# mLSTM values and output gates as one level of Strassen's product, with the 404-column group first

## What is computed

```python
hin = _rms_norm(x, norm_g[0])
z = hin @ w_in
(mq, mk, mv, lq, lk, lv, lo, li, lf,
 nq, kc, vc, ksl, vsl, kwn, vwn, ng) = jnp.split(z, split_points, axis=-1)
...
qk = jax.nn.silu(_causal_conv(jnp.concatenate([lq, lk], axis=-1), conv_w, conv_b))
```

## Time and profile before

| what | value |
|---|---|
| median of 3 runs | 603.32 us (603.21 to 603.87) |
| the profiled execution, whole | 603.88 us |
| its span, first to last instruction | 602.1 us |
| PE busy | 590.5 us (98%), 3095 matmuls |
| DVE, ACT, POOL busy | 390.1, 300.0, 257.0 us |
| mean granted TensorE clock | 0.997 of full speed |

### The profile page before, as it was taken

The page is one execution under the profiler, slowest core; times in us unless marked ns, Lnnn a source line. Parts: engine busy times, 40 slices in busy tenths (PEclk is TensorE's granted clock), DMA queues, the critical chain, the costliest instruction groups (busy, mean ns, idle before and its releaser), DMA issues.

```text
span 602.1 us, 8286 instructions
## 1 busy us (share of the span) xinstructions
PE 590.5 (98%) x3095; PEld 484.5 (80%) x3095; DVE 390.1 (65%) x666; ACT 300.0 (50%) x529; POOL 257.0 (43%) x138
## 2 busy tenths in 40 slices
PE   8999999999999999999999999999999999999995
PEld 5898888877866678899878888888888888888884
DVE  6414605266978774983999777585595685771656
ACT  6713414654589934555645545444355265354322
POOL 7763323573094610043357443631723626611611
PEclk9999999999999999999999999999999999999998
DMA  8743282466023710028034340621603404104002
GB/s 326 288 144 137 72 208 71 87 161 208 1 45 104 264 63 0 1 72 280 1 143 137 136 144 1 209 71 67 202 12 139 141 0 153 57 1 175 1 35 106
DMA packets 36580, 67.18 MB, mean 112 GB/s; under 512 B 2876, under 2 KB 23612, under 8 KB 35516
## 3 DMA queue, kind: packets, MB, share of 16 engines
q1 hardware_dynamic: 36236, 66.25, 34.0%
q10 hardware_dynamic: 304, 0.39, 0.3%
HBM read 62.18 MB, written 2.10 MB: 107 GB/s over the span
## 4 chain that ended last, share of the span: by engine, by line
PE 89%; ACT 4%; DVE 3%; issue 2%; DMA 1%; SPq 0%; POOLq 0%; POOL 0%; ACTq 0%; DVEq 0%
PE ps L1814 19%; PE ps L1816 19%; PE ps L1815 19%; PE ps L2288 7%; PE ps L2290 7%; PE ps L2289 7%; PE ps L2140 2%; PE ps L2155 2%; PE ps L2051 1%; PE ps L2052 1%; ACT probs L949 1%; DMA x_land<-in_x_turned 1%; ACT W L890 1%; PE ps L1979 1%; PE ps L2216 1%
## 5 line engine op out<-in xcount | busy, mean ns | idle before, releaser
L1814 PE MATMUL ps<-xT_h,ring_h 128*128 128x512 f32 (+1 forms) x384 | 144.3, 376 | 0.3 <-DVE q_far L1361 0.3
L1816 PE MATMUL ps<-xT_h,ring_l 128*128 128x512 f32 (+1 forms) x384 | 143.2, 373 | 0.0
L1815 PE MATMUL ps<-xT_l,ring_h 128*128 128x512 f32 (+1 forms) x384 | 143.1, 373 | 0.0
L773 POOL TENSOR_TENSOR ring_l<-raw_d,ring_h 128x1024 fp32r<-128x1024 f32 x25 | 67.3, 2699 | 129.8 <-ACT ring_h L1044 129.8
L773 POOL TENSOR_TENSOR ring_l<-raw,ring_h 128x1024 fp32r<-128x1024 f32 x31 | 76.7, 2499 | 77.5 <-DVE xres L1630 38.1
L692 POOL TENSOR_TENSOR ring_l<-raw,ring_h 128x512 fp32r<-128x512 f32 (+2 forms) x26 | 64.2, 2489 | 74.1 <-ACT ring_h L796 74.1
L1724 DVE TENSOR_TENSOR y<-ps,y 128x512 f32<-128x512 f32 x90 | 61.2, 689 | 50.9 <-PE ps L2290 50.6
L1814 PEld LDWEIGHTS ps<-xT_h,ring_h 128*128 128x128 f32 x384 | 72.4, 188 | 14.0 <-issue 1.3
L1816 PEld LDWEIGHTS ps<-xT_h,ring_l 128*128 128x128 f32 x384 | 72.3, 188 | 12.9
L1815 PEld LDWEIGHTS ps<-xT_l,ring_h 128*128 128x128 f32 x384 | 72.4, 189 | 12.5
L2288 PE MATMUL ps<-ring_h,a_h 128*128 128x512 f32 x196 | 76.7, 391 | 0.1
(11 more groups left out here) (276 smaller groups left out, 994.7 us busy)
## 6 DMA issues: line engine op xcount, KB each, us to landing
raw<-in_w_mlp SPq DMA_DIRECT2D x16, 1024.0 KB, 5.6
raw_d<-in_w_mlp SPq DMA_DIRECT2D x16, 1024.0 KB, 6.1
raw<-in_w_groups SPq DMA_DIRECT2D x8, 1024.0 KB, 4.8
xres<-in_x SPq DMA_DIRECT2D x8, 512.0 KB, 6.3
raw<-in_nsa_cmp_w SPq DMA_DIRECT2D x8, 512.0 KB, 6.6
raw<-in_w_groups SPq DMA_DIRECT2D x8, 256.0 KB, 5.5
raw<-in_w_out SPq DMA_DIRECT2D x2, 1024.0 KB, 6.2
raw<-in_w_out SPq DMA_DIRECT2D x4, 512.0 KB, 4.8
```

What stands on the lines that cost most here:

```text
L773: nc.gpsimd.tensor_tensor(slot(ring_l, n), slot_source(n), slot(ring_h, n).bitcast(F32), ALU.subtract).then_inc(lo_done, 1)
L1814: nc.tensor.matmul(o, sh, mh, start=start, stop=False)
L1815: nc.tensor.matmul(o, sh, ml, start=False, stop=False)
L1816: return nc.tensor.matmul(o, sl, mh, start=False, stop=stop)
```

## The change

`lv` and `lo` are now one product of x (1024 features by 512 tokens) with 1024 columns, done by one level of Strassen's scheme in Winograd's form. x is cut in two halves of features and two halves of tokens (`x_part`), the weights in two halves of features and two of columns: `C_11` and `C_21` are `lv`, the raw halves of `lo` land in the chunks `C_T3` and `C_22`. Eight block products become seven (`C_11`, `C_T2`, `C_21`, `C_T3`, `C_T4`, `C_T1`, `C_22`), each of 2 token tiles by 4 slabs by 3 matmuls of 512 columns. That makes 168 matmuls in place of 192.

For that VectorE makes four sums of x blocks (`s_raw`, 128x1024) and ScalarE and VectorE their halves (`s_h`, `s_l`); VectorE makes four sums of weight blocks (128x2048, `weight_sum`), and it adds the products' banks (`first_p`, `two_p`, `three_p`) before the values are scaled and the gates are formed. Three of the seven chunks are not loaded but summed. Two further raw buffers are used, `raw2` and `raw3`, and two for sums, `t_sum`.

The first group, slab by slab, is now group B with 404 columns. `x_gain` writes x back where it lies in SBUF (`x_all`), so that ScalarE's rounding and `x_low` read SBUF too; `xf` is gone. The row of scales moves on TensorE from behind group B to behind the first convolution tile, and its bank from 3 to 7. POOL makes the low halves of `LQ` and `LK` before its small constants `sel`.

```diff
-SHARED = ()
-CHUNK_ORDER = [*range(C_MQ), C_CMP + 2, C_CMP + 3, *range(C_MQ, C_CMP + 2), *range(C_WO, C_MLP)]
+C_11, C_T2, C_21, C_T3, C_T4, C_T1, C_22 = range(C_S, C_S + 7)
+SUMMED = (C_T2, C_T4, C_T1)
+CHUNK_ORDER = [C_LK, C_11, C_T3, C_22, C_21, C_KVS, C_NQ, C_CMP + 2, C_CMP + 3, C_MQ, C_MK, C_CMP, C_CMP + 1, *range(C_WO, C_MLP)]
...
+    return {C_T2: 4, C_T1: 4, C_21: 2, C_22: 3, C_CMP: 1, C_CMP + 1: 0, C_CMP + 2: 2, C_CMP + 3: 3}.get(c, c % RAW)
...
+    if C_S <= c < C_KVS:
+        return (4 if c in (C_21, C_22) else 0), 4, [(LO if c in (C_T3, C_22) else LV, 512)]
...
+                if c in (C_21, C_22):
+                    sp.wait_ge(xl_ready, NC + 3)
...
+            low_half(C_LQ)
+            low_half(C_LK)
...
+                if c in (C_T1, C_T2, C_T3, C_T4):
+                    act.wait_ge(t_ready, (C_T1, C_T2, C_T3, C_T4).index(c) + 1)
+                else:
+                    act.wait_ge(raw_in[raw_slot(c)], raw_full(c))
...
-            high_half(2)
-            for t in range(NT):
-                x_root(t)
-            for c in (3, 4, 5, 6):
-                high_half(c)
+            high_half(C_LQ)
+            x_root(0)
+            x_root(1)
+            act.wait_ge(x_scaled, NC + 4)
+            for n in (1, 2, 0):
+                sum_high(n)
+            high_half(C_LK)
+            x_root(2)
+            x_root(3)
+            high_half(C_11)
...
-                    high_half(7)
+                    high_half(C_T2)
+            high_half(C_21)
             conv_sigmoid(3)
             act.wait_ge(*reads(J_B + NT - 1))
             nc.scalar.activation(gt[:], zB[:, :, BG:BG + 12], ACT.Sigmoid).then_inc(gates_ready, 1)
-            high_half(8)
-            for t in range(NT):
-                act.wait_ge(job_done, J_LO + t + 1)
-                act.wait_ge(x_rstd, t + 1)
-                nc.scalar.activation(y[:, t, 256:768], ps[:, (J_LO + t) % 8, :], ACT.Sigmoid,
-                                     scale=stat[:, R_X + t:R_X + t + 1]).then_inc(read_a, 1)
-            high_half(9)
+            high_half(C_T3)
+            high_half(C_T4)
+            high_half(C_T1)
+            act.wait_ge(job_done, J_S + 4)
+            sum_high(3)
+            high_half(C_22)
+            high_half(C_KVS)
+            high_half(C_NQ)
+            def gate_of(t, held):
+                nc.scalar.activation(y[:, t, 256:768], held, ACT.Sigmoid, scale=stat[:, R_X + t:R_X + t + 1])
+            act.wait_ge(x_rstd, NT)
+            for t in range(2):
+                act.wait_ge(part_read, 5 + t)
+                gate_of(2 + t, three_p[:, t, :])
+            for t in range(2):
+                act.wait_ge(*reads(J_S + 6 + t))
+                gate_of(t, two_p[:, t, :])
...
             def x_gain(k):
                 dve.wait_ge(x_land_in[k], 16)
-                if k == 0:
-                    dve.wait_ge(xf_ready, 1)
-                nc.vector.tensor_scalar(ps[:, 4 + k % 4, :], x_slab(k), gain_cols[:, k:k + 1], None, ALU.mult).then_inc(x_scaled, 1)
+                nc.vector.tensor_scalar(x_all[:, k, :], x_all[:, k, :], gain_cols[:, k:k + 1], None, ALU.mult).then_inc(x_scaled, 1)
             def x_low(k):
                 dve.wait_ge(xh_ready, k + 1)
-                nc.vector.tensor_tensor(xT_l[:, k, :], ps[:, 4 + k % 4, :], xT_h[:, k, :].bitcast(F32), ALU.subtract
+                nc.vector.tensor_tensor(xT_l[:, k, :], x_all[:, k, :], xT_h[:, k, :].bitcast(F32), ALU.subtract
                                         ).then_inc(xl_ready, 1)
+            def sum_low(n, order):
+                dve.wait_ge(xh_ready, NC + order)
+                nc.vector.tensor_tensor(s_l[n][:], s_raw[n][:], s_h[n][:].bitcast(F32), ALU.subtract).then_inc(xl_ready, 1)
             x_gain(0)
             for k in range(NC):
                 if k + 1 < NC:
                     x_gain(k + 1)
                 x_low(k)
+            nc.vector.tensor_tensor(s_raw[0][:], x_part(0, 1), x_part(1, 1), ALU.add).then_inc(x_scaled, 1)
+            nc.vector.tensor_tensor(s_raw[2][:], x_part(0, 0), x_part(0, 1), ALU.subtract).then_inc(x_scaled, 1)
+            dve.wait_ge(x_scaled, NC + 1)
+            nc.vector.tensor_tensor(s_raw[1][:], s_raw[0][:], x_part(0, 0), ALU.subtract).then_inc(x_scaled, 1)
+            dve.wait_ge(x_scaled, NC + 3)
+            nc.vector.tensor_tensor(s_raw[3][:], x_part(1, 0), s_raw[1][:], ALU.subtract).then_inc(x_scaled, 1)
+            for order, n in enumerate((1, 2, 0)):
+                sum_low(n, order + 1)
             for t in range(NT):
                 normalise(t)
+            link(nc.vector.memset(lv1[:, :, :, DV:DV + 1], 1.0))
...
+            def weight_sum(c):
+                if c == C_T1:
+                    dve.wait_ge(raw_in[raw_slot(C_11)], raw_full(C_11))
+                    dve.wait_ge(raw_in[raw_slot(C_T3)], raw_full(C_T3))
+                    dve.wait_ge(x_sq, NT)
+                    made = nc.vector.tensor_tensor(t_sum[0][:], raw[1][:], raw[0][:], ALU.subtract)
+                elif c == C_T2:
+                    dve.wait_ge(raw_in[raw_slot(C_22)], raw_full(C_22))
+                    dve.wait_ge(t_ready, 1)
+                    made = nc.vector.tensor_tensor(t_sum[1][:], raw[3][:, 0:CHUNK], t_sum[0][:], ALU.subtract)
+                elif c == C_T3:
+                    made = nc.vector.tensor_tensor(raw[1][:], raw[3][:], raw[1][:], ALU.subtract)
+                else:
+                    dve.wait_ge(raw_in[raw_slot(C_21)], raw_full(C_21))
+                    dve.wait_ge(t_ready, 2)
+                    dve.wait_ge(lo_done, split_no(C_11) + 1)
+                    made = nc.vector.tensor_tensor(raw[0][:], raw[2][:], t_sum[1][:], ALU.subtract)
+                made.then_inc(t_ready, 1)
...
+                if n == 0:
+                    weight_sum(C_T1)
+                if n == 1:
+                    weight_sum(C_T2)
+                if n == 2:
+                    weight_sum(C_T3)
             silu(3)
+            weight_sum(C_T4)
+            for t in range(2):
+                dve.wait_ge(part_used, 2)
+                nc.vector.tensor_copy(first_p[t][:], ps[:, t, :]).then_inc(part_read, 1)
+            for t in range(2):
+                dve.wait_ge(part_used, 3)
+                dve.wait_ge(part_read, 1 + t)
+                nc.vector.tensor_tensor(two_p[:, t, :], ps[:, 2 + t, :], first_p[t][:], ALU.add).then_inc(part_read, 1)
+            def values_of(t, bank):
+                return nc.vector.tensor_scalar(lv1[:, t, :, 0:DV], ps[:, bank, :].rearrange("p (h d) -> p h d", h=HEADS), by_token(t),
+                                               None, ALU.mult)
+            for t in range(2):
+                dve.wait_ge(job_done, J_S + t + 1)
+                values_of(t, t).then_inc(read_v, 1)
+            for t in range(2):
+                dve.wait_ge(job_done, J_S + 2 + t + 1)
+                nc.vector.tensor_tensor(three_p[:, t, :], ps[:, 2 + t, :], first_p[t][:], ALU.add).then_inc(read_v, 1)
+            sum_low(3, 4)
+            for t in range(2):
+                dve.wait_ge(job_done, J_S + 4 + t + 1)
+                dve.wait_ge(*reads(J_S + 2 + t))
+                link(nc.vector.tensor_tensor(ps[:, 4 + t, :], ps[:, 4 + t, :], three_p[:, t, :], ALU.add))
+                values_of(2 + t, 4 + t).then_inc(read_v, 1)
+            for t in range(2):
+                dve.wait_ge(part_used, 4)
+                nc.vector.tensor_tensor(three_p[:, t, :], ps[:, 6 + t, :], three_p[:, t, :], ALU.add).then_inc(part_read, 1)
+            for t in range(2):
+                dve.wait_ge(job_done, J_S + 6 + t + 1)
+                dve.wait_ge(part_read, 3 + t)
+                nc.vector.tensor_tensor(two_p[:, t, :], ps[:, 6 + t, :], two_p[:, t, :], ALU.add).then_inc(read_v, 1)
...
+            def product(c, lh, ll, tok, bank, fresh, ends, ready):
+                wh, wl = chunk(c)
+                for t in range(2):
+                    pe.wait_ge(*ready[t])
+                    for k in range(4):
+                        cols_ = slice(tok + t * P, tok + (t + 1) * P)
+                        last = mm3(ps[:, bank + t, :], lh[:, k, cols_], ll[:, k, cols_], wh[:, k, :], wl[:, k, :], fresh and k == 0, k == 3, not fresh)
+                    if ends is job_done:
+                        last.then_inc(job_done, 1)
+                if ends is part_used:
+                    last.then_inc(part_used, 1)
+            def values_and_gates():
+                low, high = (xT_h[:, 0:4], xT_l[:, 0:4]), (xT_h[:, 4:8], xT_l[:, 4:8])
+                bank_free(J_S)
+                bank_free(J_S + 1)
+                product(C_11, *low, 0, 0, True, part_used, [reads(J_B), reads(J_B + 1)])
+                pe.wait_ge(xl_ready, NC + 1)
+                product(C_T2, s_h[1], s_l[1], 0, 2, True, part_used, [reads(J_B + 2), reads(J_B + 3)])
+                product(C_21, *high, 0, 0, False, job_done, [(part_read, 1), (part_read, 2)])
+                pe.wait_ge(xl_ready, NC + 2)
```

(26 more changed lines are left out.)

201 lines of the change are left out of this document (95 added, 106 removed).

## The result

The changed kernel takes **625.21 us** (median of six runs, 624.38 to 625.42) against 603.27 for the kernel before, measured beside it: a ratio of 1.036 with a 95% interval of 1.0347 to 1.0374. It is slower by 22 us. The forecast was slower too, with 622 us in a range of 604 to 629.

A forecast was written before the change was run, and what follows sets the result against it. TensorE, 98% busy with back-to-back matmuls, was taken as the bound. A mark 17.4 us later plus 1.5 for the clock, +18.9 on 603.9 (622.8), less 0.6 to the median, gave 622 us, range 604 to 629.

The forecast's parts named there:

- Removed, 5.4 us: TensorE's products: 24 fewer matmuls of 512 columns at 0.227 us each, all on the path, save 5.4 us.
- The slab loop: First group, now 404 columns: 2.2 us a slab, eighth slab ending at 23.7, first convolution tile at 29.1.
- I charge the gain at its old 0.65, not excluding POOL: VectorE's in-place gain in the slab loop: 0.65 us each, not blocked by POOL; eight slabs end at 18.1.
- Rival 1: In-place gain also excludes POOL, at its old length: everything behind comes 4.8 us later, 627 us; chance 0.17.
- some 2.3 us more: In-place gain by the skill's two-port rule: halved and excluding POOL, 624 us in all; not taken as main case.
- The sums and the scale row: Before the second convolution tile: x sums end at 27.3, scale row ready at 35.8, TensorE waits 6.7 us.
- The series of the turns: VectorE's convolution turns with weight sums: from 38.1, 27.1 us plus 13.0 of additions, mostly POOL exclusion.
- The wait for `first_p`: TensorE before the third product: ready at 64.6, waits 14.4 us for VectorE's copies, until 79.0.
- From there to the mark: From third product to the next group's first product: five products, copies and gap, mark at 107.8 against 90.45 before.
- the clock: After TensorE's long second wait: 2.9 us at half clock, costing 1.5 us; bounds zero to 2.7 us.
- 3 and 4: VectorE's length alone, no blocking: 602 us, chance 0.10; all hidden, TensorE saving its 5.4 us: 598 us, chance 0.11.
- Rival 2: Partial blocking: VectorE gets between POOL ops more often, 4.6 us before T4 or the sums vanishes; 609 us, chance 0.14.

The follow-up runs named there:

- order_only: Kernel before the change with only the group order changed (404-column group first), values and gates plain products, gain in PSUM: 604.44 us.
- silus_last: Changed kernel with VectorE's order behind the fourth convolution turn altered: `first_p` copies, T4's sum, `two_p`, then silus 2 and 3: 616.45 us.
- clock_held: Changed kernel with 52 small matmuls, read by nothing, between second and third product, where TensorE otherwise waits: 623.13 us.
- own_turn_psum: Changed kernel with gain in PSUM, each silu behind its own turn's weight sum, copies, T4 and `two_p` ahead of silu 3: 613.27 us.
- low_split: Changed kernel with POOL's low halves made in steps of 512 columns instead of whole 2048-column chunks: 618.44 us.
- three_together: Changed kernel with low halves in 512-column steps, `first_p` copied ahead of the last silus, and the gain in PSUM: 615.05 us.
- own_turn_psum_split: The own_turn_psum kernel with POOL's low halves additionally in steps of 512 columns: 615.08 us.

## Why the prediction was right, point by point

- **Removed, 5.4 us.** 24 matmuls fewer, as put. They shorten TensorE's path, and the waits more than take it back.
- **The slab loop.** The first convolution tile was to end at 29.1 and ended at 32.6. With the gain in PSUM and no sums (order_only) it ends at 29.5. The term that was mis-sized is "I charge the gain at its old 0.65, not excluding POOL". It is 0.47 to 0.49 alone and 1.26 to 1.32 beside POOL; `x_low` ended at 19.8, not 18.1. Slab 1 waited 1.5 us, and the clock's fall behind it made the tile another 1.4 late; no other trace here has that fall (in silus_last the tile ends at 31.5), and it cost nothing, because TensorE waits for the scale row anyway. Rival 1 had the mechanism, at a price of 4.8; measured is 2.5, for the gain and `x_low` together. The Trainium skill (VectorE: DVE Perf Modes, "Mode 2×_2P — use both read ports for one tensor") says that such an operation takes both read ports and runs at two elements a cycle, and I had worked out some 2.3 us more from it. The trace agrees on both sides: shorter alone, though not halved (0.47 to 0.49 against 0.75), and exclusive beside POOL. On this term the rule was better than my choice.
- **The sums and the scale row.** The sums were to end at 27.3 and ended at 28.9. The row was to be ready at 35.8 and was at 37.2. The first turn was to start at 38.1 and started at 40.3. The wait at the row was to be 6.7 and is 4.6, because TensorE itself came 3.5 later to it. Both sides are late, so the wait came out 2 us short, and the first turn 2.2 us late.
- **The series of the turns.** 27.1 plus 13.0 of additions from 38.1; measured 38.8 from 40.3 to 79.1. The total was right within 1.3 us, and in part by luck, since **the places were wrong**: T1 was charged 1.3 and met 0.4, silu 3 and T4 were charged 4.4 and 4.6, and in fact silus 2 and 3 took 8.7 together and T4 nothing. Silu 1's 1.5 and the `conv_linear`'s 1.2 came as put (1.4 and 1.2). It made no difference to the time, but it would have sent the remedy to the weight sums' blocking, of which there was 0.4 us in all.
- **The wait for `first_p`.** 14.4 forecast, 13.5 measured; the third product at 79.0 forecast, 79.9 measured.
- **From there to the mark.** 28.8 and 1.5 for the clock forecast, 31.7 measured. The clock was mis-sized: it came back only after 5.3 us of matmuls, not 2.9, and 12 x 0.2 = 2.4 us; clock_held confirms it. The upper bound was too low as well: 2.7 us is what 5.4 us of time at half clock lose, while the 24 matmuls of a product at 0.43 instead of 0.23 would lose 4.8. That the half clock behind the first wait hides was right. The other 0.5 us of this stretch I did not trace.
- **Rivals.** 3 and 4 are refuted by every silu and sum that met a low half on POOL. Rival 2 holds in part: the 4.6 in front of T4 did fall away, as it has it, but silu 2 was caught in its place. The two engines take turns by whole instructions: VectorE got in once between the two low halves.
- **The balance.** Forecast 622, measured 625.2. The first turn came 2.2 us late, the series was 1.3 shorter, so that the third product came 0.9 late; from there to the mark 1.4 more, of which 0.9 is the clock; 0.4 behind the mark; and the rest of 0.5 comes from setting the profiled execution against the median. The two mis-sized terms, gain and clock, are larger than the miss, since the shorter series took a part back.

**What stays open.** In own_turn_psum the mark is at 99.45, 9.0 us behind the kernel before, and 24 matmuls are missing, so that 14.4 us have to be explained. The distances between the starts of TensorE's matmuls give 13.9 of them: the first tile begins 1.6 late against order_only; the scale row holds TensorE up for 3.3; the wait for `ring_l` takes 4.9 and the one for `three_p` 1.1; and behind the two long waits matmuls at half clock lose 1.3 and 1.7. For the 10 us that are left of the changed kernel's 22 there are thus only these rows; no run here removes them. Whether another arrangement of the sums (on another engine, or as other blocks) would bring the product below 603 was not tried, nor was a kernel with the weight sums left out and nothing in their place.

## What to carry to other kernels

Count a product's saved matmuls against all that the sums ask of the engine that makes them: here 24 matmuls (5.4 us) cost 43.7 us of VectorE, blocked time and the gain's change included, and brought it onto the chain. When two engines shut each other out by whole instructions, look for the short instruction between two long ones of the other engine and at what stands behind it in line: moving the copies ahead of two silus of 0.6 us gave back 7.4 of 22 us, and 9.1 with the last sum ahead of them too. Before a run that replaces an instruction, look up how long the replacement takes: the memsets were nearly as long as the sums, so that run could not price them. A total that comes out right is no proof that its parts are.

## What the hardware showed that I had not expected

- A float32 `tensor_scalar` from SBUF to SBUF in place, 512 columns, takes 0.47 to 0.49 us against 0.75 into PSUM, but 1.26 to 1.32 beside a POOL instruction of about 1.1 us with two SBUF inputs.
- The granted clock is not the same from execution to execution. After the wait of 13.5 us it stayed at 0.50 for 5.3 us of matmuls without a gap. Behind the scale row it was back at 40.8 in the changed kernel and only at 43.4 in silus_last, whose queues are the same up to there. Behind a wait of 1.5 us at slab 1 it was 0.51 in the changed kernel's trace and 1.00 in low_split's.
- A VectorE memset of 2048 float32 columns has a row of 1.76 us with some 0.4 us of idle time before it that no wait explains. The two together are 2.1 to 2.2 us, as long as a two-input sum's 2.2 from start to start.
- Cutting POOL's 2048-column instruction in four made LQ's low half 7.4 to 8.5 us (three_together, own_turn_psum_split, low_split) instead of 5.1 to 5.6 beside VectorE's sums: each cut is an entry for the other engine.
